# Input projection of a hybrid decoder step by seven block products per pair of weight tiles

## The reference

```
u    = rmsnorm(x)                       # 536 x 1024
proj = u @ w_in                         # 1024 x 5888: 46 tiles of 128 output columns
# 14 tiles: RWKV-7 r, k, v and the decay / a / gate LoRA inputs, each lerped with the token before
# 16 tiles: retention q, k, v, g (4 heads of 128)
# 16 tiles: logits of the two branch gates
kk = heads(k * k_k);  kk = kk / max(sqrt(sum(kk * kk, per head of 64)), 1e-12)
o  = o * rsqrt(mean(o * o) + eps);  o = silu(g_r) * o          # retention output, per head
merged = sigmoid(g_a) * (ya @ w_branch_a) + sigmoid(g_b) * (o @ w_branch_b)
x = x + merged @ w_out;  x = x + hierarchical_moe(rmsnorm(x));  y = rmsnorm(x)
```

## Time and profile before

| | |
|---|---|
| median of 3 runs | 868.27 us |
| span of the profiled execution, first to last instruction | 864.1 us |
| TensorE busy | 833.3 us, 96%, 9014 records |
| VectorE busy | 367.7 us, 43% |
| ScalarE busy | 183.5 us, 21% |
| GpSimd busy | 33.2 us, 4% |
| chain that ended last | TensorE 89% of the span, L1038 (input projection) 44% |

### The profile page before, as it was taken

The page is one execution under the profiler, slowest core; times in us unless marked ns, Lnnn a source line. Parts: engine busy times, 40 slices in busy tenths (PEclk is TensorE's granted clock), DMA queues, the critical chain, the costliest instruction groups (busy, mean ns, idle before and its releaser), DMA issues.

```text
span 864.1 us, 20515 instructions
## 1 busy us (share of the span) xinstructions
PE 833.3 (96%) x9014; PEld 588.4 (68%) x9014; DVE 367.7 (43%) x731; ACT 183.5 (21%) x418; POOL 33.2 (4%) x31
## 2 busy tenths in 40 slices
PE   7999999999999999999999999998999959999994
PEld 5877777787788777777777777766878733333331
DVE  6343343337788554554552333316412252111036
ACT  2101111143312212112211231212003141111135
POOL 0000000000000000000000000000000011122221
PEclk9999999999999999999999999999999969999998
DMA  9431231413121111011113010019192479999965
GB/s 350 162 101 62 94 109 58 173 50 121 49 74 61 39 39 39 27 41 39 39 40 100 27 52 27 27 26 379 36 383 102 158 265 425 383 394 394 393 227 188
DMA packets 29912, 124.21 MB, mean 144 GB/s; under 512 B 5656, under 2 KB 8248, under 8 KB 24960
## 3 DMA queue, kind: packets, MB, share of 16 engines
q1 hardware_dynamic: 25936, 113.03, 35.0%
q0 software_dynamic: 3888, 9.87, 4.1%
HBM read 106.31 MB, written 18.68 MB: 145 GB/s over the span
## 4 chain that ended last, share of the span: by engine, by line
PE 89%; DMA 3%; DVE 3%; ACT 2%; issue 2%; SPq 1%; POOL 0%; POOLq 0%; ACTq 0%; DVEq 0%
PE psum L1038 44%; PE psum L1349 9%; PE psum L2139 8%; PE psum L2171 4%; PE psum L1171 2%; PE psum L1210 2%; PE psum L1305 1%; PE psum L1223 1%; PE psum L2119 1%; PE psum L1127 1%; PE psum L1115 1%; PE psum L1220 1%; PE psum L1191 1%; PE psum L1140 1%; DMA u_rows<-arena 1%
## 5 line engine op out<-in xcount | busy, mean ns | idle before, releaser
L1038 PE MATMUL psum<-arena 128*128 128x268 f32 x1600 | 396.1, 395 | 0.7 <-DVE arena L1643 0.5
L1038 PEld LDWEIGHTS psum<-arena 128*128 128x128 f32 x1600 | 292.4, 189 | 74.8 <-issue 12.6
L1640 DVE TENSOR_TENSOR arena<-psum,arena 128x256 f32<-128x256 f32 (+6 forms) x178 | 75.0, 426 | 202.8 <-PE psum L1223 52.8
L1443 ACT ACTIVATE arena<-psum 128x268 f32<-128x268 f32 (+6 forms) x184 | 71.4, 396 | 369.5 <-PE psum L1038 271.3
L1640 DVE TENSOR_TENSOR arena<-arena 128x256 f32<-128x256 f32 (+11 forms) x204 | 102.1, 501 | 43.3 <-ACT arena L1443 31.0
L1349 PE MATMUL psum<-arena 128*128 128x268 f32 x384 | 90.5, 390 | 0.9 <-DVE arena L1643 0.9
L2139 PE MATMUL psum<-arena 128*32 128x512 f32 (+1 forms) x640 | 85.7, 597 | 0.5 <-DVE arena L2292 0.3
L1349 PEld LDWEIGHTS psum<-arena 128*128 128x128 f32 x384 | 71.2, 189 | 16.3 <-DVE arena L1643 1.7
L2292 DVE TENSOR_TENSOR arena<-psum,arena 128x256 f32<-128x256 f32 (+2 forms) x38 | 24.3, 663 | 104.8 <-ACT arena L2206 90.8
L2139 PEld LDWEIGHTS psum<-arena 128*32 128x32 f32 (+1 forms) x640 | 25.1, 115 | 57.5 <-issue 56.9
L1643 DVE SCALAR_TENSOR_TENSOR arena<-arena 128x8 f32<-128x8 f32 (+6 forms) x93 | 49.0, 527 | 12.3 <-DMA arena<-arena 9.1
(11 more groups left out here) (195 smaller groups left out, 670.8 us busy)
## 6 DMA issues: line engine op xcount, KB each, us to landing
arena<-in_w_gu SPq DMA_DIRECT2D x16, 2048.0 KB, 21.3
arena<-in_w_in SPq DMA_DIRECT2D x46, 512.0 KB, 3.5
arena<-in_w_dn SPq DMA_DIRECT2D x16, 1024.0 KB, 19.8
arena<-in_w_out SPq DMA_DIRECT2D x2, 2048.0 KB, 12.6
arena<-in_x SPq DMA_DIRECT2D x8, 268.0 KB, 5.2
arena<-arena SPq DMA_DIRECT2D x16, 134.0 KB, 3.3
arena<-in_x SPq DMA_DIRECT2D x1, 2144.0 KB, 13.0
arena<-in_rets SPq DMA_DIRECT2D x1, 2048.0 KB
```

Source lines behind the costliest of these rows:

```text
L1038: last = mm(ps, wt[:, i % NW, k, :], rhs[:, k, cols(hf)], start=(k == 0), stop=(k == nk - 1))
L1443: run(nc.scalar.activation(out, in_, fn, **kw), s)
L1640: run(v.tensor_tensor(out, a, b, op), s)
```

## The change

Of the 46 tiles of `w_in`, the q and k tiles of head 0 and the 16 gate tiles stay as they were. The other 28 are made in 14 pairs (`PAIRS`). For a pair (A, B), the two tiles, the two halves of the 1024 input rows (4 blocks each) and the two halves of tokens form a 2 x 2 by 2 x 2 block product, and Winograd's form of Strassen's scheme needs seven block products of 4 matmuls for it, not eight. For it there are

- four combinations of the activations, once (`tk`, DVE, 4 x 268 columns each);
- four combinations of the weights per pair (`pair_sum`: s1 = b_lo + b_hi, s2 = s1 + a_lo, b_lo = b_lo + a_lo, s4 = a_hi + s2, 512 columns each; signs are in the activations' combinations), all on GpSimd (`ON_POOL` holds every pair), each waiting for the one before to end;
- seven jobs `("j_w", n, i)`; 2, 4, 5 and 6 go on adding in the bank of the job two before, after ACT has copied what stood there;
- seven evacuations by ACT and three additions `wa` on DVE, with buffers `m1`, `us`, `m5`.

Weights come by pairs (`pair(n)`, two DMAs of 512 KB) into two sets of buffers; pair n is issued when pair n-2 is done. The steps of attention are placed anew at job numbers b, where b 0 to 3 are the jobs of q and k of head 0 and pair n has b = 4 + 7n to 10 + 7n; phase 2 counts b from 0 again. `orn` of heads 0 to 2 is moved from phase 2 into phase 1. The gates are copied plain; their sigmoid (`gsig`) and products (`gmul`) stand in phase 2. The shift is done once a tile is assembled. Key norms: `j_kks` gathers the sums of all four p into 4 x 32 rows of one bank (4 products of 32 columns), one square root, maximum and reciprocal (`kkr`) per half follow, and `j_kkb` spreads them again (2 products of 64 columns per p and half), multiplied in from PSUM.

The core of the diff:

```diff
+PAIRS = [(RET0 + 8, RET0 + 1), (RET0 + 5, RET0 + 9), (RET0 + 2, RET0 + 6), (RET0 + 10, RET0 + 3),
+         (RET0 + 7, RET0 + 11), (RET0 + 12, RET0 + 13), (RET0 + 14, RET0 + 15),
+         (12, 13), (4, 5), (6, 7), (0, 1), (2, 3), (8, 9), (10, 11)]
+NRP = 7
+SEVEN = 7
+BEHIND = {1: 0, 4: 1, 5: 2}
+ON_POOL = set(range(len(PAIRS)))
...
+    def seven(n, after):
+        out = []
+        for i in range(SEVEN):
+            out.append(("j_w", n, i))
+            if i in BEHIND:
+                out.append(("wa", n, BEHIND[i]))
+            if n + 1 < len(PAIRS):
+                out += [("ws", n + 1, k) for k in {3: [0], 4: [1], 5: [2], 6: [3]}.get(i, [])]
+            out += after.get(i, [])
+        return out
...
+    at_k = [0, 2, 3, 5, 6, 8, 9, 10]
+    for h, b in enumerate((11, 21, 32, 42)):
         n = h * NB_H
...
+        for k in range(1, 8):
+            then(b + at_k[k], *[("att", n + x) for x in at_slot.get(k - 1, [])],
+                 *[("j_score", n + x) for x in at_slot.get(k, [])])
+        then(b, ("j_vt", h), ("j_t4", h), ("rs_v", h))
+        then(b + at_k[1], ("j_kt", h))
+        then(b + at_k[2], ("rs_a", h))
+        then(b + at_k[4], ("rs_b", h))
+        then(b + at_k[6], ("j_ros", h))
+    for b, j in ((5, 0), (7, 4), (13, 1), (19, 5), (26, 2), (28, 6), (33, 3), (39, 7)):
+        then(b, ("rope", j))
+    for h, b in enumerate((24, 34, 46)):
+        then(b, ("osq", h))
+        then(b + 1, ("j_orms", h, 0), ("j_orms", h, 1))
+        then(b + 3, ("orn", h))
...
+    then(1, ("osq", RH - 1), ("phase2",))
+    then(2, ("j_orms", RH - 1, 0), ("j_orms", RH - 1, 1))
     for h in range(RH):
+        then(4 + h, ("gsig", h))
+    then(5, ("orn", RH - 1))
+    for h in range(RH):
+        then(8 + h, ("gmul", h))
+    then(10, ("lora_in",))
     for p in range(NP):
+        then((16, 18, 22, 24)[p], ("kk_in", p))
         for hf in range(2):
+            then(12 + 3 * p + hf, ("j_lora", "w", p, hf), ("j_lora", "a", p, hf))
+            then(30 + p + 4 * hf, ("j_kkb", p, hf))
+            then((39, 41, 43, 45)[p], ("j_lora", "g", p, hf))
+        then((15, 19, 23, 25)[p], ("scan", p))
+        then((39, 41, 43, 45)[p], ("bon_in", p))
+    then(26, ("j_kks", 0), ("j_kks", 1))
+    then(28, ("kkr", 0))
+    then(29, ("kkr", 1))
...
+            def one_of_seven(n, i):
...
+                w, x = [(a[:, lo], quarter["b11"]), (a[:, hi], quarter["b21"]), (s2, t2n), (s1, t1n), (b[:, lo], t3),
+                        (s4, quarter["b22"]), (b[:, hi], t4)][i]
+                for k in range(KD // 2):
+                    last = mm(ps, w[:, k, :], x[:, k, :], start=(k == 0 and i in (0, 1, 3)), stop=(k == KD // 2 - 1),
+                              skip_group_check=i not in (0, 1, 3))
+                last.then_inc(s_job, 1)
...
+            for n in sorted(ON_POOL):
+                for k in range(4):
+                    sum_ready(pool, n, k)
+                    nc.gpsimd.tensor_tensor(*pair_sum(n, k), ALU.add).then_inc(s_sum[1], 1)
+                    sums += 1
+                    pool.wait_ge(s_sum[1], sums)
...
+                elif kind == "j_w":
+                    _, n, i = step
+                    if n and i in (0, 2, 3):
+                        act.wait_ge(s_asm, 3 * n - 3 + {0: 1, 2: 3, 3: 2}[i])
...
+                    job_done(act, step)
+                    out = [m1, made(n, 0, 0), us, m5, made(n, 1, 1), made(n, 0, 1), made(n, 1, 0)][i]
+                    f(out, job_ps(step), s=free, scale=-1.0 if i in (4, 6) else 1.0)
...
+                    if (k, p, hf) == ("w", 0, 0):
+                        act.wait_ge(s_on, RH)
```

More of the change, by code:

```diff
@@ new lines, in order @@
+    for b, j in ((5, 0), (7, 4), (13, 1), (19, 5), (26, 2), (28, 6), (33, 3), (39, 7)):
[4 more added lines that the diff above has]
+        then(b + 3, ("orn", h))
+    s = [("sq", 0), ("sq", 1), ("j_norm", 0, 0), ("j_norm", 0, 1)]
+    s += [("tk", i) for i in range(4)]
+    b = 0
+    for hf in range(2):
+        for m in (RET0, RET0 + RH):
+            s += [("j_proj", m, hf)] + behind.get(b, [])
+            b += 1
+        if hf == 0:
+            s += [("ws", 0, k) for k in range(4)]
@@ L195, in prep @@
+    for n in range(NRP):
+        s += seven(n, {i: behind.get(b + i, []) for i in range(SEVEN)})
+        b += SEVEN
     def prep(c, *what):
         return [(k, c, i) for k, i in what] if c < len(CHUNKS) else []
[L198 to L203, removed]
+    behind.clear()
+    then(1, ("osq", RH - 1), ("phase2",))
+    then(2, ("j_orms", RH - 1, 0), ("j_orms", RH - 1, 1))
     for h in range(RH):
-        put(h // 2, h % 2 if h < 2 else h % 2, ("j_orms", h, 0), ("j_orms", h, 1))
@@ new lines, in order @@
+        then((39, 41, 43, 45)[p], ("bon_in", p))
+    then(26, ("j_kks", 0), ("j_kks", 1))
+    then(28, ("kkr", 0))
+    then(29, ("kkr", 1))
+    then(46, ("wk_e", 0), *prep(0, ("wk_p", 0), ("wk_p", 1), ("wk_p", 2), ("wk_p", 3), ("wk_d", 0), ("wk_d", 1)))
+    for n in range(NRP, len(PAIRS)):
+        after = {i: behind.get(SEVEN * (n - NRP) + i, []) for i in range(SEVEN)}
+        after[6] = [("shift", PAIRS[n][0])] + after[6]
+        if n > NRP:
+            after[0] = [("shift", PAIRS[n - 1][1])] + after[0]
+        s += seven(n, after)
@@ L221, in order @@
+    s += [("shift", PAIRS[-1][1]), ("st0",)]
     fill = []
@@ L477, in hybrid_step, with fill_tile @@
         shd = at(SHIFT_TILES * NB, SHIFT_TILES, NB, start=smp0 + SHIFT_TILES * NB)
+        def fill_tile(i):
+            return at(1024, KD, P, start=SLOTS_AT[1] + 1024 * i) if i < NW else wt[:, i % NW]
         def k_tok(h, t0, t1, rows=P):
@@ L509, in hybrid_step @@
         s_w = [sem(f"s_w{i}") for i in range(NW)]
+        s_wp = [sem(f"s_wp{i}") for i in range(2)]
+        s_sum = {i: sem(f"s_sum{i}") for i in range(2) if (len(ON_POOL) if i else len(ON_POOL) < len(PAIRS))}
+        s_asm = sem("s_asm")
         s_job = sem("s_job")
@@ new lines, in _ @@
+            pair(0)
+            sp.dma_start(s_new, I["rets0"]).then_inc(s_rets, 16)
+            turned(0)
+            pair(1)
+            turned(RH)
+            pair(2)
+            turned(1)
+            kept(0)
+            pair(3)
+            turned(RH + 1)
+            kept(1)
+            pair(4)
+            turned(2)
+            turned(RH + 2)
+            pair(5)
+            turned(3)
+            kept(2)
+            pair(6)
+            turned(RH + 3)
+            kept(3)
+            pair(7)
@@ L949, in _ @@
+            sp.wait_ge(s_sn, RH)
+            sp.wait_ge(s_roq, RH)
+            sp.dma_start(O["rets"], s_new).then_inc(s_out, 16)
+            pair(8)
+            sp.wait_ge(s_ph, 1)
+            sp.dma_start(ws, I["wkv0"]).then_inc(s_rets, 16)
+            for n in range(9, len(PAIRS)):
+                pair(n)
+            for i in range(len(WTILES)):
                 weights(i)
-                if NW <= i < NW + 3 * RH and (i - NW) % 3 < 2:
-                    turned((i - NW) // 3 + RH * ((i - NW) % 3))
@@ L1029, in products @@
                 ps = job_ps(step) if part else open_job(step)
+                if m in (RET0, RET0 + RH) and kind == "j_proj":
+                    i = (m - RET0) // RH
+                    if hf == 0:
+                        pe.wait_ge(s_w[i], 16)
+                    for k in range(nk):
+                        if i == 0:
+                            pe.wait_ge(s_u, KD * hf + k + 1)
+                        last = mm(ps, wt[:, i, k, :], rhs[:, k, cols(hf)], start=(k == 0), stop=(k == nk - 1))
+                    last.then_inc(s_job, 1)
+                    return
@@ L1422, in _, with shift_at @@
                     positions(0)
-        SHIFT_ORDER = [s_[1] for s_ in STEPS if s_[0] == "j_proj" and s_[1] < SHIFT_TILES and s_[2] == 0]
+        SHIFT_ORDER = [s_[1] for s_ in STEPS if s_[0] == "shift"]
+        def shift_at(m):
+            n = [i for i, ab_ in enumerate(PAIRS) if m in ab_][0]
+            return n, PAIRS[n].index(m)
         def shifted(m):
@@ L1744, in _ @@
                     dve.wait_ge(s_att, len(RB))
[L1745 removed]
+                    for x in raws:
+                        run(v.memset(x[:, :, 0:1], 0.0), s_ph if x is raws[1] else None)
                     run(v.memset(ep[:, :, :, 0:1], 1.0))
                     run(v.memset(psum[:, 3328:3584], 0.0))
+                elif kind == "st0":
                     run(v.memset(st[:, 0], 0.0), s_st)
```

317 lines of the change are left out of this document (190 added, 127 removed).

## The result

The changed kernel takes 878.09 us (median of 4 runs, 877.4 to 878.37) against 867.78 of the kernel before in the same series: ratio 1.0124, interval 1.011 to 1.0138. It is slower by 10 to 11 us, where 12 us faster was forecast; 878 lies above the whole range of 847 to 868.

A forecast was written before the change was run, and what follows sets the result against it. TensorE, busy without a gap up to 284 us, was taken as the bound: 25.3 off, 4.3 on for key norms, 6.2 on for waits, 2.5 on for GpSimd, so 12.3 us off; 856.0 us, range 847 to 868.

The forecast's parts named there:

- Seven products, 25.3 us off: Input projection on TensorE: seven half-length jobs per pair replace four, 112 matmul records fewer, 25.3 us off.
- D: Rival: accumulating onto an evacuated bank or half-length jobs costs TensorE 0.2 us a job; 868, within the 0.05 for same.
- Key norms, +4.3: TensorE: eight full jobs go, two sum jobs and eight spreading jobs come; net 4.3 us on.
- The tight places, +6.2: TensorE waits for late VectorE: head 1 2.2, head 2 0.9, head 3 0.8, phase 2 gates 1.6, first spreading job 0.7.
- the gates' place: Jobs 5 to 15 of phase 2: VectorE's queue lags and LoRA inputs cost ScalarE 3.9 us; TensorE waits 1.6 us.
- GpSimd on VectorE, +2.5 between 0 and 10.5: What GpSimd's sums cost by disturbing VectorE while both read SBUF: 2.5 us on, bounds zero and 10.5.
- the upper bound: Every sum meeting VectorE in places 1, 2, 4 and head 2's first rope stops it: seven x 1.5 = 10.5 us.
- the only row: Tail, GpSimd busy with DMA instructions: VectorE's two-input operation took 1.26 ns a column against 1.36 elsewhere, no stretch.
- B: Rival: VectorE and GpSimd block each other for whole sums at ropes and gate multiplies; 4.3 us off, 864; chance 0.21.
- C: Rival: slow, fully blocking sums make VectorE the bound of phase 2; 880 at 2.3 us a sum; chance within slower's 0.11.
- The 0.11 for slower: Chance given to C and other slower ends together, against 0.84 for faster and 0.05 for same.

The follow-up runs named there:

- e1: The changed kernel with each of GpSimd's 48 sums from pair 2 on cut to one column; 858.1 us, ratio 0.9909 to the kernel before.
- e9: e7 with each rope's row swap queued ahead of its weight pair and the key norms' spreading jobs two by two; 848.9 us, ratio 0.9786 to the kernel before.
- e5: The changed kernel reordered: normalisations of heads 0 to 2 later, gate sigmoids and products earlier, decay and a-gate jobs two jobs later; 866.7 us.
- e10: e9 with all 56 sums back on GpSimd; 855.1 us, ratio 0.985 to the kernel before.
- e7: The changed kernel with all sums on VectorE, the order of e5 and the LoRA inputs at job 12 instead of 10; 854.5 us.
- e8: The changed kernel with GpSimd, from pair 2 on, writing a constant instead of each sum and reading nothing; 859.0 us, ratio 0.990 to the kernel before.

## Why the prediction was wrong

- **The sum at the start of the recurrence.** The forecast puts it at 292.2 - 12.3 = 279.9, and at 277.4 without the term for GpSimd. It is 302.4, and 280.8 in e1, where GpSimd's reading is nearly gone. So 19 of the 22.5 us of error lie in that one term (21.7 for 2.5), and about 3 in all the others.
- **Seven products, 25.3 us off.** Right. The job of 8 records takes the predicted 1.81 us at the full clock (85.72 to 87.53 us), and e9 starts the recurrence at 272.8. D was dead with e1.
- **Key norms, +4.3.** Right for the form in the change: a job and a spreading job take 257.02 to 259.64 us, 2.62, so 0.81 for the spreading job, predicted 0.8.
- **The tight places, +6.2.** Right where the port is out of play: e1's waits are 2.04 at head 1 (predicted 2.2), 0.98 at head 2 (0.9), 2.00 at the gates (1.6), and 6.1 in all. Head 3 and the spreading job did not wait there (0.8 and 0.7 predicted); small waits elsewhere took their place. In the working of the gates' place one piece was wrong: the LoRA inputs need no table load behind the gates' sigmoids and take ScalarE 1.19 us, not 3.9; the wait comes from VectorE's queue alone.
- **GpSimd on VectorE, +2.5 between 0 and 10.5: the step that failed.** The mechanism of the upper bound was right, and so was the length of a sum (1.41 us, I took 1.5). The cost to VectorE was mis-sized: it was worth 12.9 us of waits and, with the clock that fell behind them, 21.7. I went by the only row in which both engines were at work, though I had written down that those were DMA instructions; a row without an addition of GpSimd was no evidence for one. And the upper bound of 10.5 was too low: I counted seven sums that meet VectorE in tight places, but stretched operations made VectorE late in places that were not tight by the price list: head 2's first attention product (2.6), a second LoRA job (4.3), the first job that waits for the activations (0.6).
- **The clock: missing from the sum.** I let every wait count its own length. Behind the waits of 4.48, 2.60, 3.29 and 4.30 us the clock stood at its lower level for the next jobs, and a wait of 4.5 us cost about 7. Every wait of over 3 us in these runs was followed by such a fall; of those between 1.7 and 2.7 us some were (2.65 in e5, 2.00 at the gates in e1, 2.42 and 1.70 in e10) and some not (2.47 in e5, 2.27 in e7). Head 1's wait is 2.04 us in both e1 and e8; the clock fell behind it in e8 alone. What tells these apart stays open. The 8.8 us by which e1 gains more than its waits are nearly all this term.
- **The rivals.** B's mechanism is the one that came, sums that stop VectorE where ropes and gate steps stand, with too small a price (864). That the time is near C's 880 is luck. C lets VectorE become the bound of phase 2, and that needs sums of 2.3 us. At the measured 1.41 its own formula gives 79 + 24 x 1.41 = 113 us against 108, or 858 us. Phase 2 was not saturated (VectorE was busy 93 of 127 us there), and phase 1, where C had nothing, lost more: its waits are 12.3 of the 19.0 us. The 0.11 for slower was too little for a term that no row of the trace could size.

## What to carry to other kernels

Before work is given to GpSimd because it is idle, look at what VectorE does at that time: if its operations take two operands from SBUF (here a tensor_scalar was caught too), the sum on VectorE itself (0.69 us a sum) can be cheaper than on GpSimd (1.41 us, in which VectorE may stand). When the jobs of the bounding engine get shorter, the slack of every evacuation shrinks with them (here, by the prediction's estimate, from 2.9 to 1.1 us), and long operations (a reciprocal of 3.5 us) must be moved out of the queue ahead of whatever it waits for. A wait of several microseconds on TensorE is to be priced with the slow jobs behind it.

## What the runs showed that was not expected

Packing four small norms into one bank costs TensorE 0.81 us a spreading job alone and 0.62 in twos. A memset of 128 x 512 by GpSimd takes 532 ns and leaves VectorE alone; an addition of the same size takes 1410. ScalarE needed two table loads from 16 to 290 us in the changed kernel, against six from 16 to 285 before: tanh ran in the table that the gates' sigmoids had loaded (189.89 us; the LoRA inputs at 204.43 have no load), while before tanh and the sigmoid behind it had one load each.
